# A gated delta rule with the triangular solve moved from the preparation of a head into its scan

## The reference: what is computed

```python
M = jnp.where(strict, bc[..., :, None] * kk * decay_in, 0.0)
rhs = jnp.concatenate([bc[..., None] * vc, (bc * jnp.exp(G))[..., None] * kc], axis=-1)
sol = lax.linalg.triangular_solve(M + eye, rhs, left_side=True, lower=True)
u_v, w_k = sol[..., :DV], sol[..., DV:]
...
def step(S, xs):
    u = u_v_n - jnp.einsum('bhld,bhdv->bhlv', w_k_n, S)
    o = jnp.einsum('bhld,bhdv->bhlv', q_dec_n, S) + jnp.einsum('bhij,bhjv->bhiv', qk_n, u)
    S = S * g_last_n[..., None, None] + jnp.einsum('bhld,bhlv->bhdv', k_dec_n, u)
```

## Time and profile before

| | |
|---|---|
| time, median of 3 runs | 1744.55 us (1744.27 to 1745.53) |
| the profiled execution: its span, first to last instruction | 1743.5 us (no other time was recorded for it) |
| median above that span | 1.05 us |
| TensorE busy | 94% of the span |
| VectorE busy | 63% |
| ScalarE busy | 42% |
| GpSimd busy | 9% |
| mean granted TensorE clock | 0.977 of full speed |

### The profile page before, as it was taken

One profiled execution on the slowest core, in us unless ns is written; L12 is line 12 of the kernel. 1 busy time (PEld: TensorE's weight loads), 2 busy tenths in 40 slices (PEclk: granted clock), 3 DMA queues, 4 the chain that ended last, 5 costly groups with the idle time before them and its releaser, 6 DMA issues. The chain is left out here.

```text
span 1743.5 us, 30855 instructions
## 1 busy us (share of the span) xinstructions
PE 1638.5 (94%) x11642; PEld 1418.0 (81%) x11643; DVE 1099.3 (63%) x2286; ACT 729.1 (42%) x1376; POOL 165.4 (9%) x160
## 2 busy tenths in 40 slices
PE   5999999999999999999998999999999989999990
PEld 3899999999999989778874799999987855666650
DVE  6587787878778782666546221035349866777756
ACT  5656454554545442445444332122121114444434
POOL 0100000000000001000000000000000004344430
PEclk9999999999999999999999999999999989999995
DMA  9211202021120201523409321123323359988866
GB/s 368 75 48 54 77 18 81 25 82 41 54 81 17 79 16 55 203 91 134 154 1 326 125 80 55 43 72 107 121 91 102 143 219 354 323 274 264 262 164 218
DMA packets 68194, 222.11 MB, mean 127 GB/s; under 512 B 10812, under 2 KB 16724, under 8 KB 62436
## 3 DMA queue, kind: packets, MB, share of 16 engines
q1 hardware_dynamic: 57892, 183.41, 29.1%
q0 software_dynamic: 10176, 36.97, 8.0%
HBM read 180.50 MB, written 42.48 MB: 128 GB/s over the span
## 5 line engine op out<-in xcount | busy, mean ns | idle before, releaser
L145 PE MATMUL banks<-hT_high,w_high 128*128 128x352 f32 x840 | 294.6, 351 | 2.9 <-ACT raw L778 2.0
L147 PE MATMUL banks<-hT_high,w_low 128*128 128x352 f32 x840 | 272.0, 324 | 0.0
L146 PE MATMUL banks<-hT_low,w_high 128*128 128x352 f32 x840 | 271.8, 324 | 0.0
L145 PEld LDWEIGHTS banks<-hT_high,w_high 128*128 128x128 f32 x840 | 159.6, 190 | 10.6 <-issue 3.3
L146 PEld LDWEIGHTS banks<-hT_low,w_high 128*128 128x128 f32 x840 | 160.1, 191 | 0.0
L147 PEld LDWEIGHTS banks<-hT_high,w_low 128*128 128x128 f32 x840 | 159.1, 189 | 0.0
L1146 DVE SCALAR_TENSOR_TENSOR f<-raw,cw,f 128x1059 f32<-128x1059 f32 x72 | 96.7, 1344 | 36.0 <-ACT UV L854 35.7
L145 PE MATMUL pg<-hT_high,w_high 128*128 128x352 f32 x360 | 116.2, 323 | 0.8 <-PEq L1500 0.8
L146 PE MATMUL pg<-hT_low,w_high 128*128 128x352 f32 x360 | 115.4, 320 | 0.0
L147 PE MATMUL pg<-hT_high,w_low 128*128 128x352 f32 x360 | 115.3, 320 | 0.0
L2874 PE MATMUL psD<-wdn,aTx 128*128 x192 | 87.0, 596 | 2.3 <-DVE ob L3006 1.6
(11 more groups left out here) (485 smaller groups left out, 4043.6 us busy)
## 6 DMA issues: line engine op xcount, KB each, us to landing
wgu<-in_w_gu SPq DMA_DIRECT2D x16, 2048.0 KB, 8.1
wraw<-in_w_gdn SPq DMA_DIRECT2D x32, 512.0 KB, 3.6
wdn<-in_w_dn SPq DMA_DIRECT2D x16, 1024.0 KB, 12.9
spare<-in_w_mod SPq DMA_DIRECT2D x15, 512.0 KB, 8.2
wm<-in_w_mod SPq DMA_DIRECT2D x6, 1024.0 KB, 13.3
Dm<-tmp_g_rows SPq DMA_DIRECT2D x8, 576.0 KB, 5.5
EG<-tmp_g_rows SPq DMA_DIRECT2D x8, 576.0 KB, 6.5
tmp_ya<-yat SPq DMA_DIRECT2D x8, 528.0 KB, 2.8
```

The source lines that it names most:

```text
L145: pe.matmul(out, lh, rh, start=start, stop=False)
L146: pe.matmul(out, lh, rl, start=False, stop=False)
L147: return pe.matmul(out, ll, rh, start=False, stop=stop)
```

## The change

The inverse T is kept (`TT`) and applied in the scan. The stages WK and UV go, with their evacuations and with the multiplication of the keys by beta and decay. In their place slot n makes z = k S (L1121's place), VectorE makes `rest` = b v - b e^G z in one instruction out of PSUM, TensorE makes v = T rest, and VectorE copies it from its PSUM bank to SBUF as u. What follows u is as before. Slot 0 makes v = T(b v) and its u. The filler steps of a slot are split into three parts (2, 2, 2; in pass 6: 2, 1, 1) for the three places between TensorE's products, and the shares of the filler are spread over nine stages. The keys' copy `ks` for the scan is made by ScalarE in stage C; `qd` holds the decayed queries that were in half of `WE`; `bv` gets a buffer of its own.

VectorE's pieces keep their places: the first piece of a slot now stands between `rest` and the copy of u, the second behind the state.

```diff
-    A2 = ("QK", "C", "Z1", "Z2", "ZI", "X", "T_O", "T_V", "TX", "WK", "UV")
-    SHARE = {"QK": 4, "C": 5, "Z1": 5, "Z2": 5, "ZI": 4, "T_O": 3, "X": 4, "T_V": 3, "TX": 4, "WK": 3, "UV": 3}
+    A2 = ("QK", "C", "Z1", "Z2", "ZI", "X", "T_O", "T_V", "TX")
+    SHARE = {"QK": 5, "C": 5, "Z1": 5, "Z2": 5, "ZI": 5, "T_O": 4, "X": 5, "T_V": 4, "TX": 5}
...
-        return (hi - lo + 1) // 2, (hi - lo) // 2
+        return (hi - lo + 2) // 3, (hi - lo + 1) // 3, (hi - lo) // 3
...
-                            if stage == "WK":
-                                for g in range(NGRP):
-                                    src = take_from(act, a, "WK", g)
-                                    act.activation(WE[:, G3 * g:G3 * g + G3, 0:P], src[:, 0:W3].rearrange("p (t n) -> p t n", n=P),
-                                                   ACT.Copy).then_inc(free[g], 1)
-                            if stage == "UV":
-                                evacuate(a, "UV", UV)
+                            if stage == "C":
+                                act.wait_ge(s["actv"], 3 * a + 1)
+                                if a > 0:
+                                    act.wait_ge(s["ds"], NCHUNK * a)
+                                act.activation(ks[:, :], f[KB][:, :], ACT.Copy).then_inc(s["ks"], 1)
...
-                    if name == "WK":
-                        pe.wait_ge(s["kb"], a + 1)
-                        evacuated(pe, a, "TX")
-                        stage(a, "WK", mul(kt, TT))
-                    if name == "UV":
-                        evacuated(pe, a, "T_V")
-                        stage(a, "UV", mul(TT, bv))
...
                         if n == 0:
 
+                            evacuated(pe, h, "TX")
+                            pe.matmul(sw[:, 2 * P:3 * P], tl(TT, 0), tl(bv, 0), start=True, stop=True).then_inc(s["v"], 1)
+                            run(fill, fills[0] + fills[1])
                             pe.wait_ge(s["kd"], h + 1)
...
+                            pe.wait_ge(s["S"], NCHUNK * h + n)
+                            pe.matmul(sw[:, 0:P], tl(ks, n), Sn, start=True, stop=True).then_inc(s["z"], 1)
+                            pe.wait_ge(s["o_taken"], NCHUNK * h + n + 1)
+                            pe.matmul(out[:, 0:P], tl(qd, n), Sn, start=True, stop=False)
+                            run(fill, fills[0])
+                            pe.wait_ge(s["rest"], (NCHUNK - 1) * h + n)
+                            pe.matmul(sw[:, 2 * P:3 * P], tl(TT, n), rest[:, :], start=True, stop=True).then_inc(s["v"], 1)
+                            run(fill, fills[1])
+                        pe.wait_ge(s["u"], NCHUNK * h + n + 1)
+                        pe.matmul(sw[:, P:2 * P], tl(kd, n), u[:, n % 2, :], start=True, stop=True).then_inc(s["ds"], 1)
...
+                        pe.matmul(out[:, 0:P], tl(PT, n), u[:, n % 2, :], start=(n == 0), stop=True).then_inc(s["o"], 1)
+                        run(fill, fills[2])
...
-                            dve.tensor_tensor(by_tile(kt), by_tile(kt), col[:, 2, :].unsqueeze(2).to_broadcast([P, TILES, P]),
-                                              ALU.mult).then_inc(s["kb"], 1)
...
+                def solved(h, n):
+                    dve.wait_ge(s["v"], NCHUNK * h + n + 1)
+                    dve.tensor_copy(u[:, n % 2, :], sw[:, 2 * P:3 * P]).then_inc(s["u"], 1)
...
                         if n == 0:
+                            solved(h, 0)
                             next(part, None)
                             dve.wait_ge(s["ds"], NCHUNK * h + 1)
                             dve.tensor_copy(S[1][:, :], sw[:, P:2 * P]).then_inc(s["S"], 1)
                             next(part, None)
                             continue
-                        dve.wait_ge(s["ws"], (NCHUNK - 1) * h + n)
-                        dve.tensor_tensor(u[:, n % 2, :], tl(UV, n), sw[:, 0:P], ALU.subtract).then_inc(s["u"], 1)
+                        dve.wait_ge(s["z"], (NCHUNK - 1) * h + n)
+                        dve.scalar_tensor_tensor(out=rest[:, :], in0=sw[:, 0:P], scalar=nbeg[:, h % 2, n:n + 1], in1=tl(bv, n),
+                                                 op0=ALU.mult, op1=ALU.add).then_inc(s["rest"], 1)
                         next(part, None)
+                        solved(h, n)
```

More of the change, by code:

```diff
@@ L65 @@
 V_ORDER, V_THR, V_CHUNK, V_PAIR = 16, 20, 32, 72
-Q_G, Q_CUM, Q_NBETA, Q_BETA, Q_BEG, Q_KD, Q_GL0, Q_GL1 = range(8)
+Q_G, Q_CUM, Q_NBETA, Q_BETA, Q_NBEG, Q_KD, Q_GL0, Q_GL1 = range(8)
 NQ = 8
@@ L615, in phase_deltanet @@
         yat = buf("yat", [P, PAD])
-        Dm, EG, ET, C, TT, kt, kd, PT, UV = (buf(n, [P, PAD]) for n in
-                                             ("Dm", "EG", "ET", "C", "TT", "kt", "kd", "PT", "UV"))
+        Dm, EG, ET, C, TT, kt, kd, PT, bv = (buf(n, [P, PAD]) for n in
+                                             ("Dm", "EG", "ET", "C", "TT", "kt", "kd", "PT", "bv"))
         RT, R = (buf(n, [P, TILES * HB2]) for n in ("RT", "R"))
         HALVES = (slice(0, HB2), slice(HB2, P))
-        WE = buf("WE", [P, TILES, 2 * P])
-        we = WE[:, :, :].rearrange("p t c -> p (t c)")
+        qd, ks = buf("qd", [P, PAD]), buf("ks", [P, PAD])
         WZ = TILES * HB2
         NB, CR = C[:, 0:WZ], C[:, WZ:2 * WZ]
-        Z1, Z2, XL = we[:, 0:WZ], we[:, WZ:2 * WZ], we[:, 2 * WZ:3 * WZ]
-        IV, bv, sqq = UV[:, 0:WZ], ET, kt
+        Z1, Z2, XL = qd[:, 0:WZ], qd[:, WZ:2 * WZ], NB
+        IV, sqq = bv[:, 0:WZ], kt
         blk = buf("blk", [P, BS, BS])
@@ L638, in phase_deltanet @@
         u = buf("u", [P, 2, P])
+        rest = buf("rest", [P, P])
+        nbeg = buf("nbeg", [P, 2, TILES])
         c1 = buf("c1", [P, BS])
@@ L649, in phase_deltanet @@
             "actv", "sq", "rows_in", "eg_in", "dm_min", "dm", "cols", "rk", "blk_in", "x_raw", "x_off", "x_in",
-            "x_one", "x_done", "rt", "r", "kd", "kb", "eq", "st_in", "S_out", "y_out", "tail_out",
-            "ws", "u", "ds", "S", "o", "o_taken", "ms", "rms", "on", "chain",
+            "x_one", "x_done", "rt", "r", "kd", "ks", "eq", "st_in", "S_out", "y_out", "tail_out",
+            "z", "rest", "v", "u", "ds", "S", "o", "o_taken", "ms", "rms", "on", "chain",
             "nt", "y_in", "y_act", "g_made", "cum", "e_in", "e_done", "gcol", "growT", "grow", "grow_out")}
@@ L849, in prep @@
                     x.then_inc(s["r"], 1)
-                def evacuate(a, stage, dst):
-                    for g in range(NGRP):
-                        src = take_from(act, a, stage, g)
-                        act.activation(grp(dst, g), src[:, 0:W3], ACT.Copy).then_inc(free[g], 1)
                 def evacuate_upper(a, stage, dst):
@@ L908, in _ @@
                                 evacuate_upper(a, "TX", lambda g: grp3(TT, g)[HALVES[0], :, HB2:P])
-                            if stage == "WK":
-                                for g in range(NGRP):
-                                    src = take_from(act, a, "WK", g)
-                                    act.activation(WE[:, G3 * g:G3 * g + G3, 0:P], src[:, 0:W3].rearrange("p (t n) -> p t n", n=P),
-                                                   ACT.Copy).then_inc(free[g], 1)
-                            if stage == "UV":
-                                evacuate(a, "UV", UV)
+                            if stage == "C":
[3 more added lines that the diff above has]
+                                act.activation(ks[:, :], f[KB][:, :], ACT.Copy).then_inc(s["ks"], 1)
                             if stage == "T_V" and a + 1 < HA:
+                                act.wait_ge(s["ks"], a + 1)
                                 tap(a + 1, KB)
@@ L1093, in _ @@
                     for n in range(SLOTS):
-                        before, behind = slot_steps(h, n)
+                        fills = slot_steps(h, n)
                         if h < 0:
-                            run(fill, before + behind)
+                            run(fill, sum(fills))
                             next(part, None)
@@ L1100, in _ @@
                         if n == 0:
+                            evacuated(pe, h, "TX")
+                            pe.matmul(sw[:, 2 * P:3 * P], tl(TT, 0), tl(bv, 0), start=True, stop=True).then_inc(s["v"], 1)
+                            run(fill, fills[0] + fills[1])
                             pe.wait_ge(s["kd"], h + 1)
-                            evacuated(pe, h, "UV")
+                            evacuated(pe, h, "QK")
                             pe.wait_ge(s["S"], NCHUNK * h)
-                            pe.matmul(sw[:, P:2 * P], tl(kd, 0), tl(UV, 0), start=True, stop=True).then_inc(s["ds"], 1)
@@ L1106, in _ @@
-                            run(fill, before)
-                            evacuated(pe, h, "QK")
-                            pe.wait_ge(s["o_taken"], NCHUNK * h + 1)
[L1109 to L1128, removed]
+                        else:
+                            if n == 1:
+                                pe.wait_ge(s["ks"], h + 1)
```

(27 more changed lines are left out.)

## The result

The changed kernel takes 1761.28 us (median of 4 runs, 1759.28 to 1762.41), the kernel before 1745.04 us beside it (4 runs, 1744.27 to 1746.36). The ratio is 1.0095 (95% interval 1.008 to 1.0109): slower by 16.2 us. The profiled execution of the changed kernel is the fastest of its runs, 1759.28 us with a span of 1757.3 us, 13.8 more than the span before.

A forecast was written before the change was run, and what follows sets the result against it. TensorE bounds passes 0 to 5, VectorE the slots of pass 6. Passes 0 to 5 +13.4, pass -1 -4.1, pass 7 +2.0, pass 6 +3.0 make +14.3 us: 1758.9 us, range 1746 to 1774, likeliest case 1752 to 1767.

The forecast's parts named there:

- The products: TensorE, each head: two stages removed save 4.07 us, nine added products v cost 2.03; -16.3 us in all without waits.
- The chain of a slot: Passes 0 to 5: three handovers per slot, two filler steps each; overlong VectorE pieces make TensorE wait 4.27 us a pass.
- restart: TensorE, any matmul that had to wait: it takes 0.49 instead of 0.39 us, so each wait costs 0.10 more.
- Pass -1: The pass without a scan: only the removed stages count, -4.1 us.
- Pass 7: The pass that prepares nothing: VectorE has no pieces, no bound breaks, +2.0 us.
- Pass 6: VectorE stays the bound: slots +8.8 us, less 4.1 for stages, 0.8 ahead of C and 0.9 for clock; +3.0.
- my walk: Timing followed slot by slot with VectorE's pieces; in pass 6 it shortened the 2.08 us wait before C by 0.8.
- The second step: Pass 6, stretch at clock 0.95: half of the 1.9 us lost to the clock, 0.9 us, counted as returned.
- The clock rival: New waits bring the lower clock once in each of seven passes, 1.9 us each: 1772 us; chance 0.13.
- The sum: Whole kernel: 13.4 - 4.1 + 2.0 + 3.0 = +14.3 us; span 1757.8, median 1.05 above it, 1758.9.

The follow-up runs named there:

- the mixed kernel: Changed kernel, passes 0 to 5 filler placed by pieces; ScalarE copies u in slots 7 and 8 and all of passes 6 and 7: 1732.37 us, ratio 0.9929.
- the last run: The mixed kernel with ScalarE spreading the inverses' blocks ahead of filler evacuation and weight copy in slot 8 of pass 6: 1731.95 us, ratio 0.9935.
- the two kernels with the same instructions at 1.00: Changed kernel with ScalarE copying u in every slot, without and with new filler splits in slots 0 and 4 of passes 0 to 5: 1749.73 and 1744.23 us.

## Why the prediction was right, and where a size was off

The sign, the size (1758.9 forecast, 1761.28 measured) and the mechanism in passes 0 to 5 were right; pass 6 was not, and misses of other sign make the total nearer than its parts (see the sum). By its steps:

**The products.** With the waits taken away the saving shows: in the mixed kernel a pass is 1.67 us shorter than before, where the products alone are worth 4.07 - 2.03 = 2.04.

**The chain of a slot.** It holds wait by wait (the prediction speaks of five slots that break the bounds; its list, and the trace, have six). In pass 2, by the distances above, with 0.10 for each restart as forecast:

| place | forecast | measured, with restart |
|---|---|---|
| slot 1, `rest` and u | 0.89 + 0.25 | 0.90 + 0.25 |
| slot 4, u | 0.13 | 0.13 |
| slot 5, `rest` | 0.44 | 0.40 |
| slot 6, u | 1.03 | 1.04 |
| slot 7, u | 0.44 | 0.50 |
| slot 8, u | 1.09 | 1.16 |
| sum | 4.27 | 4.38 |

So a pass costs 2.03 + 4.38 - 4.07 = 2.34 more; measured 2.33 (78.08 against 75.75), forecast 2.23. The copy and `rest` last 0.288 and 0.350 us in the median, as priced. The experiments show the cause: taking a piece away removes the wait beside it, the same work added costs nothing where the bound is kept and its full time where it is broken, and filler put beside the long pieces takes the loss back.

**Pass -1.** -4.1 was forecast. From the start of stage C to slot 0 it is 25.10 us before (117.70 to 142.80) and 19.87 after (114.63 to 134.50): -5.2. Two waits in front of T_V and TX, with 0.49 and 0.18 us of idle time, which the forecast had not seen, went too; with their restarts they are most of the 1.1 us over the forecast. Another 3.1 us lie ahead of stage C, half of them ahead of the phase and half in a stretch at a lower clock; no part of the change is there, and I do not count them to it. The other runs bear this out: in all nine changed kernels it is 19.9 us from C to slot 0, while C starts anywhere from 112.1 to 118.4.

**Pass 7.** +2.5 for +2.0. Its slots hold no waits, as forecast, and each of them takes 0.22 us longer; the tail behind the last increment is not shorter for the filler step that stands ahead of it now.

**Pass 6: the term that was mis-sized.** +3.0 was forecast, +6.25 measured. From slot 0 to C it takes 48.61 us instead of 36.31, +12.3 where the forecast had +8.0 (+8.8 less 0.8): +1.4 up to the first `rest`, as forecast, +9.5 from there to the last state for the 7.4 (607.89 to 645.88, where the earlier trace rows have 600.84 to 629.37), and +1.4 from the last state to C for the -0.8. Behind C it is 23.19 instead of 29.23, -6.0 for the -5.0 (4.1 and 0.9). Two steps failed. The first, and the larger with 2.2 us, is "the last u now stands behind the last transposes, which shortens the 2.08 us wait in front of C ... by my walk 0.8". It did not shorten; TensorE's timeline in pass 6 after:

```profile
608.29 0.49 PE L1111 MATMUL banks<-rest,TT 128*128 128x128 f32 x2 [1.11 <-DVE rest L1400]
...
609.72 0.63 PE L1114 MATMUL banks<-u,kd 128*128 128x128 f32 x2 [0.46 <-DVE u L1380]
...
645.36 0.49 PE L1114 MATMUL banks<-u,kd 128*128 128x128 f32 x2 [1.62 <-DVE u L1380]
...
651.61 1.26 PE L985 MATMUL banks<-R,C 64*64 64x64 f32 x36 [2.09 <-issue]
```

The wait of 2.08 us is 2.09 now. ScalarE's timeline has the reason:

```profile
646.59 0.46 ACT L772 ACTIVATE zs<-banks 128x352 f32<-128x352 f32 x1 [0.22 <-PE banks L147]
646.95 1.05 ACT L761 ACTIVATE w_high<-wraw 128x1024 fp32r<-128x1024 f32 x1
647.90 1.78 ACT L844 ACTIVATE RT<-blkT 32x288 f32<-32x288 f32 x4
649.71 1.80 ACT L848 ACTIVATE R<-blk 32x288 f32<-32x288 f32 x4
```

My walk followed VectorE only. But C needs R, which ScalarE spreads in eight copies, and it began them at 647.90, 2.8 us behind the transposes, because filler evacuation and weight copy stood in front; the last run showed that even without these two the copies keep C waiting. The second step is "I count half of its 0.05 x 37 = 1.9 us, 0.9, as returned". The stages did come at clock 1.00 instead of 0.95, and gave back the whole of it and not the half; but the slots fell from 1.00 to 0.96. The loss moved and did not grow: 0.05 of 37.00 us before, 0.04 of 43.40 now, both some 1.8. The mixed kernel gives a price for it: from slot 0 to the last increment of pass 6 it took 38.24 us with one such fall, and 36.69 and 36.66 in the two kernels with the same instructions at 1.00, so 1.6. In the kernel after, the fall begins in slot 1, with the `ds` of 609.72 above; between 609 and 614 us the clock is 0.66 in the mean, and VectorE waits there for z of slot 2:

```profile
614.79 0.35 DVE L1400 SCALAR_TENSOR_TENSOR rest<-banks,nbeg,bv 128x128 f32<-128x128 f32 x1 [1.62 <-PE banks L1106]
```

That most of the 2.1 us which the slots take over the forecast is this fall is worked out from these rows; no run repeats the kernel after with the slots at 1.00.

**The clock rival.** In passes 0 to 5 it did not come: six to seven waits of up to 1.06 us a pass, and a granted clock of 1.00. The Trainium skill (TensorE: Matmul & The Clock Gate, section "A second HAM failure mode: psum-queue depth-cycling") tells of a bf16 kernel in which short idle moments, often repeated, made the clock swing. The traces of these fp32 passes do not agree with it: 1.00 in all six. Pass 6 is where the rival had a part (above, and at the end).

**The sum.** Measured parts: 6 x 2.33 + 6.25 + 2.5 - 5.2 = +17.5 us, against +16.2 between the medians and +14.3 forecast: pass 6 is 3.25 over its forecast, and the small misses of the others cancel. The spans differ by 13.8; the 3.1 us ahead of stage C and 0.6 behind the delta rule account for what is missing there. So it is luck that the profiled span, 1757.3 us, came so close to the forecast's 1757.8: time that the change does not touch hid the miss in pass 6. The step from span to median was off too, 3.98 us where the forecast took 1.05.

## What to carry to other kernels

When work is moved from a stage into a loop with strict order, count the handovers of an iteration and give each its own bound: the filler beside it, less the other engine's start and its instruction; the pieces of that engine must fit under each bound, not under their sum. Where one breaks, move the filler before moving the work: here the order of the filler alone was worth 2.75 us a pass. An engine that is half idle on average is a free place for a wait only in those slots where nothing that others wait for stands behind it.

## What the runs showed of the hardware that was not expected

The granted clock of TensorE followed neither the number of waits nor their length alone. Passes 0 to 5 kept 1.00 (the upper level, 2.4 GHz) in every kernel here, with idle times up to 0.92 us at a wait in the kernel after and 1.12 in the kernel with extra work in slots 6 and 8. The slots of pass 6 fell to 0.96 in the kernel after, in slot 1, behind idle times of 1.11 and 0.46 us, and not at the longest wait, 1.62 us, in slot 8. They fell at the same place with the filler moved and with extra work in slots 2 and 5 (0.96 both) or 6 and 8 (0.88, with further falls); with the elimination steps left out they stayed at 1.00, though the same 1.11 and 0.46 us stand there. With ScalarE's copy, pass 6 fell twice in the mixed kernel, behind an idle time of 1.64 us in the slots and at C behind 2.07, and stayed at 1.00 in three other kernels, two of which hold the same waits. Its 69.17 us against their 66.13 and 66.10 put the price of the two falls at about 3 us. So the lower clock came behind idle times that were also there without it; each number is of one execution, and what decides stays open.
